# Shifted rows added in DRAM by an accumulating DMA, and the sample tile's first pages spread over four steps

## The reference

```python
proj = rms_norm(x) @ w_in            # 1024 -> 3328 columns: q, k (512 each), v (512), p (1792)
# attention group: causal differential attention, sample rows also over 512 cached rows by pages
# RWKV group:
p_prev = concat([shift0, p[:-1]])    # the row before; state_shift for the first row of a sequence
ps = p + (p_prev - p) * mu           # token shift
r, k, v, xw, xa, xg = split(ps)      # then decay, gates and the recurrence of a 64x64 state per head
h = x + concat(o_attention, o_rwkv) @ w_out
# retrieval: product keys choose 16 of 16384 experts for each of 8 heads and each row
h = h + sum_k gate_k * gelu(u[e_k] . hn) * v[e_k]
y = rms_norm(h)
```

## Time and profile before

| | |
|---|---|
| median of 3 runs | 3914.06 us (3906.76 to 3920.62) |
| the profiled execution | 3911.12 us |
| its span, first to last instruction | 3909.4 us |
| instructions | 54667 |
| busy | PE 73%, DVE 66%, POOL 35%, PEld 34%, ACT 33% |
| mean granted TensorE clock | 0.801 |
| moved by DMA | 1431.65 MB, mean 366 GB/s |

### The profile page before, as it was taken

How to read it: one execution, slowest core, us unless ns; L and a number is a source line. 1 busy time by engine, 2 the same in 40 slices (tenths; PEclk the granted TensorE clock), 3 DMA queues, 4 the chain that set the end, 5 groups by cost and what they waited for, 6 DMA issues and landing times. The chain is left out here.

```text
span 3909.4 us, 54667 instructions
## 1 busy us (share of the span) xinstructions
PE 2869.6 (73%) x20366; PEld 1341.9 (34%) x20366; DVE 2584.4 (66%) x5804; ACT 1294.6 (33%) x3597; POOL 1378.3 (35%) x1190
## 2 busy tenths in 40 slices
PE   8899999785767676767676776778676758867564
PEld 3654554342323223322332243224322315421121
DVE  2441563489578848884987598668866876446954
ACT  1321111325243424343344324432433234422222
POOL 1000000344344424443433343444333455643453
PEclk9899999787878787787878787877787767767665
DMA  7645335899999999999999999999999999999998
GB/s 253 225 149 217 138 142 196 316 420 419 423 410 420 419 422 409 411 420 420 412 414 405 419 412 392 408 418 393 394 414 390 375 361 405 408 403 422 417 400 357
DMA packets 254825, 1431.65 MB, mean 366 GB/s; under 512 B 27520, under 2 KB 45456, under 8 KB 110304
## 3 DMA queue, kind: packets, MB, share of 16 engines
q0 software_dynamic: 163232, 1162.26, 72.9%
q1 hardware_dynamic: 91328, 265.89, 18.0%
HBM read 1373.21 MB, written 54.85 MB: 365 GB/s over the span
## 5 line engine op out<-in xcount | busy, mean ns | idle before, releaser
L1039 POOL DMA_INDIRECT pe_buf<-in_experts,pe_idx x1088 | 1291.1, 1187 | 2364.9 <-PE pe_psO L1465 1637.7
L2312 DVE CUSTOM_DVE_ANT_0 pe_buf<-pe_buf,pe_hnR 128x1024 f32<-128x1024 f32 x1088 | 1316.7, 1223 | 702.2 <-DMA pe_buf<-in_experts,pe_idx 673.4
L1465 PE MATMUL pe_psO<-pe_buf,pe_Z 128*32 128x256 f32 x8704 | 847.6, 486 | 649.6 <-ACT pe_Z L1744 619.7
L1738 ACT ACTIVATE pe_gelu<-pe_dot 128x1 f32<-128x1 f32 x1088 | 219.2, 201 | 1634.4 <-DVE pe_dot L2312 1586.0
L1465 PEld LDWEIGHTS pe_psO<-pe_buf,pe_Z 128*32 128x32 f32 x8704 | 213.7, 123 | 1316.6 <-ACT pe_Z L1744 1006.0
L1447 PE MATMUL pe_psH<-pe_hn,pe_pick 128*128 128x512 f32 x544 | 409.8, 845 | 44.8 <-ACT pe_hnR L1720 39.8
L1076 PE MATMUL ip_B<-ip_w,ip_xT 128*128 128x512 f32 (+1 forms) x1008 | 426.4, 575 | 5.6 <-DMA ip_w<-in_w_in 5.6
L1744 ACT ACTIVATE pe_Z<-pe_gl,pe_gelu 128x8 f32<-128x8 f32 x1088 | 327.3, 301 | 46.4 <-issue 3.3
L1411 PE MATMUL pe_B<-op_wkr,pe_mix 128*128 128x512 f32 (+1 forms) x576 | 270.7, 615 | 7.4 <-DMA op_wkr<-scratch_wk_rows 7.0
L1076 PEld LDWEIGHTS ip_B<-ip_w,ip_xT 128*128 128x128 f32 x1008 | 190.5, 194 | 204.7 <-issue 200.3
L1447 PEld LDWEIGHTS pe_psH<-pe_hn,pe_pick 128*128 128x128 f32 x544 | 107.4, 243 | 174.9 <-issue 92.3
(11 more groups left out here) (343 smaller groups left out, 3577.6 us busy)
## 6 DMA issues: line engine op xcount, KB each, us to landing
op_wkr<-scratch_wk_rows SPq DMA_DIRECT2D x36, 2048.0 KB
ip_w<-in_w_in SPq DMA_DIRECT2D x18, 2048.0 KB, 8.3
op_w<-in_w_out SPq DMA_DIRECT2D x9, 2560.0 KB
pe_buf<-in_experts,pe_idx POOLq DMA_INDIRECT x1088
op_w<-in_w_out SPq DMA_DIRECT2D x9, 1024.0 KB
ip_w<-in_peer_wq SPq DMA_DIRECT2D x4, 2048.0 KB, 10.1
scratch_wk_rows<-wk_wkc SPq DMA_DIRECT2D x16, 512.0 KB, 3.0
tm_ps<-scratch_moved_rows SPq DMA_DIRECT2D x8, 896.0 KB
```

The source lines that it names most:

```text
L1039: pool.indirect_dma_start(buf[b][:], None, T["experts"], bass.IndirectOffsetOnAxis(ap=idx[:, t % 2, h * NJ + j:h * NJ + j + 1], axis=0)).t ...
L1465: last = nc.tensor.matmul(psO[32 * x:32 * x + 32, j // 4, :], Z[:, n % NZ, 24 - 8 * turn:56 - 8 * turn], buf[home[n]][:, D + x * QUART:D + ...
L1738: nc.scalar.activation(gelu[:, col:col + 1], dot[:, col:col + 1], ACT.Gelu_apprx_tanh).then_inc(f["gelu_done"], 1)
L2312: nc.vector.tensor_tensor_reduce(buf[b][:, 0:D], buf[b][:, 0:D], hnR[:, n // PH % 2, :], 1.0, 0.0, ALU.mult, ALU.add, dot[:, n % (NBUF + E ...
```

## The change

It has two parts.

The first adds the shifted rows in DRAM. For each projection unit with n of 3 to 6 POOL issues a DMA (`add_moved`) that reads the unit's block of `moved_rows` and adds it to the block of `kept_rows`; for the sample tile there are two, since the first row of each sequence comes from `moved_shift`. Each waits for the stores of its unit, for tile 0 also for `edge_stored`, and for the completion of all such DMAs before it (`added_of`). `load_p` is then one load of `ps` from `kept_rows`, behind the additions of its tile's last unit (`mixed_of`), all at step 25 of `op`; VectorE's addition and the semaphore value `MIXED` are gone, and three engines wait for the load itself. The sample tile's other constants are loaded at step 29, as before.

The second is about the sample tile's pages: the 16 page DMAs stand at leading steps 6, 7, 8 and 9, four in each, and the scaling of the queries at leading step 7.

```diff
+    def added_of(units):
+        return 16 * sum(1 if t < LAST else 2 for t, n in UNITS[:units] if n >= NV)
+    def mixed_of(t):
+        return added_of(last_unit(t) + 1)
...
                     if i == IP_FIRST + 2:
                         sp.wait_ge(at["lam_dots"], 1)
-                        sp.wait_ge(ip["edge_stored"], 32)
                         load_p(0)
...
             def load_p(t):
                 R = rows_of(t)
-                if t < LAST:
-                    load_moved(t)
-                    load_kept(t)
-                else:
-                    ... (p, eight blocks of ps, moved_shift, six constants)
+                sp.wait_ge(ip["mixed"], mixed_of(t))
+                sp.dma_start(ps[0:R], kept_rows[rows(t, R), :]).then_inc(s["p_in"], 16)
...
+            def add_moved(g):
+                t, n = UNITS[g]
+                cols = slice((n - NV) * IG, (n - NV) * IG + cols_of(n))
+                for i in range(2):
+                    pool.wait_ge(ip_stored[i], stored_of(g + 1, i))
+                if t == 0:
+                    pool.wait_ge(ip["edge_stored"], 32)
+                if added_of(g):
+                    pool.wait_ge(ip["mixed"], added_of(g))
+                if t < LAST:
+                    pool.dma_start(kept_rows[rows(t), cols], moved_rows[t * P:(t + 1) * P, cols], accum_op=ALU.add
+                                   ).then_inc(ip["mixed"], 16)
+                    return
+                ... (the same in two DMAs for the sample tile)
...
                 for k in range(SB_LEAD):
-                    if k == SB_LEAD - 1:
+                    if k == SB_LEAD - 4:
                         pool.wait_ge(at["pidx_ready"], 1)
                         pool.wait_ge(s["state_stored"], 32)
-                        for b in range(2):
-                            pages_of(kp, "cache_k", kp_in, b)
-                            pages_of(vp, "cache_v", vp_in, b)
+                        pages_of(kp, "cache_k", kp_in, 0)
+                    if k == SB_LEAD - 3:
+                        pages_of(vp, "cache_v", vp_in, 0)
+                    if k == SB_LEAD - 2:
+                        pages_of(kp, "cache_k", kp_in, 1)
+                    if k == SB_LEAD - 1:
+                        pages_of(vp, "cache_v", vp_in, 1)
                     yield
...
-                            dve.wait_ge(s["p_in"], 32 + 32 * t if t < LAST else 32 * PT + 160)
-                            nc.vector.tensor_tensor(ps[0:R], ps[0:R], p[0:R], ALU.add).then_inc(s["dve_part"], 1)
                         if k == 6:
-                            dve.wait_ge(s["dve_part"], ND * t + MIXED)
+                            dve.wait_ge(s["p_in"], 16 * (t + 1))
```

More of the change, by code:

```diff
@@ L313, in peer @@
     FIRST_IN, CONSTS_IN, TM_CONSTS_IN = 2, 7, 15
-    NA, ND = 9, 4
+    NA, ND = 9, 3
     LO_TANH, LO_READY, KK_SQUARED, LO_COPIED, KK_ROOT, G_COPIED, ZA_TANH, LW_READY, E_READY = range(1, 1 + NA)
-    MIXED, KK_SCALED, KK_SUM, SCALED = range(1, 1 + ND)
+    KK_SCALED, KK_SUM, SCALED = range(1, 1 + ND)
     def begin(t):
@@ L624, in peer @@
             gate_ready""")
-        ip = sems("ip", "summed squared scaled turned xT done rotated copied split mu_in shifted edge_stored")
+        ip = sems("ip", "summed squared scaled turned xT done rotated copied split mu_in shifted edge_stored mixed")
         ip_rope_in = [m.sem(f"ip_rope_in{i}") for i in range(MOST)]
@@ L753, in fold_stored, with load_sample_consts @@
                     sp.wait_ge(wk_stored[i], 16 * PH)
[L755 to L761, removed]
             def load_p(t):
                 R = rows_of(t)
-                if t < LAST:
-                    load_moved(t)
-                    load_kept(t)
-                else:
[L770 to L778, removed]
+                sp.wait_ge(ip["mixed"], mixed_of(t))
+                sp.dma_start(ps[0:R], kept_rows[rows(t, R), :]).then_inc(s["p_in"], 16)
+            def load_sample_consts():
+                for dst, n in ((sstate, "state"), (seq_of, "seq_of"), (seq_row, "seq_row"), (cum, "cum_s"), (tot, "tot_s"),
+                               (tri, "tri_s")):
+                    sp.dma_start(dst[:], T[n]).then_inc(s["sstate_in"], 16)
             def load_w_out(part):
@@ L877, in project_out @@
                         sp.wait_ge(op["hn_stored"], 16 * (t + 1))
-                        if t + 1 < LAST:
-                            load_moved(t + 1)
-                    if k == 29 and t < LAST:
+                        load_p(t + 1)
+                    if k == 29 and t + 1 == LAST:
                         sp.wait_ge(op["scores_done"], NC * t + NC - 1)
[L882 to L885, removed]
+                        load_sample_consts()
                     yield
@@ L979, in project @@
                         constants()
+                    if 2 <= i < len(IP) + 2:
+                        kind, g, q_ = IP[i - 2]
+                        if kind == "unit" and q_ == 1 and UNITS[g][1] >= NV:
+                            add_moved(g)
                     yield
+            def add_moved(g):
[11 more added lines that the diff above has]
+                    return
+                kept = kept_rows[rows(LAST, SROWS), cols].rearrange("(b s) n -> b s n", s=ST)
+                moved = moved_rows[1 + SEQ:1 + SEQ + SROWS, cols].rearrange("(b s) n -> b s n", s=ST)
+                pool.dma_start(kept[:, 1:ST, :], moved[:, 0:ST - 1, :], accum_op=ALU.add).then_inc(ip["mixed"], 16)
+                pool.dma_start(kept[:, 0, :], moved_shift[:, cols], accum_op=ALU.add).then_inc(ip["mixed"], 16)
             def mix_in_time(t):
@@ L1142, in mix_in_time @@
                             pe.wait_ge(s["act_part"], NA * t + LW_READY)
-                            pe.wait_ge(s["dve_part"], ND * t + MIXED)
+                            pe.wait_ge(s["p_in"], 16 * (t + 1))
                             nc.tensor.matmul(B[0:R, 0, :], cum[0:R, 0:R], lw[0:R, :], start=True, stop=True)
@@ L1532, in mix_in_time @@
                         if k == 6:
-                            act.wait_ge(s["dve_part"], ND * t + MIXED)
+                            act.wait_ge(s["p_in"], 16 * (t + 1))
                             nc.scalar.activation(lo[0:R, 0:64], ps[0:R, 3 * W:3 * W + 64], ACT.Tanh)
@@ L2126, in attend_sample @@
                                               ).then_inc(at["copied"], 1)
-                    yield
-                for k in range(SB_STEPS * (SB - 1) + SB_LONG):
-                    if k == 0:
+                    if k == 7:
                         dve.wait_ge(at["turned"], 2 * NT)
@@ L2137, in attend_sample @@
                         last.then_inc(at["copied"], 1)
+                    yield
+                for k in range(SB_STEPS * (SB - 1) + SB_LONG):
                     for b in range(SB):
```

## The result

The changed kernel takes 3922.50 us in the median of 20 runs (3916.96 to 3932.32), the kernel before 3907.14 in 20 runs (3897.70 to 3920.62): a ratio of 1.0039, interval 1.0032 to 1.0045, and a difference of 15.4 us. The change makes the kernel slower. The profiled execution of after took 3924.76 us with a span of 3923.0, against 3911.12 and 3909.4 before, 13.6 us more. The fill and the gather phase moved in opposite directions, each by more than I had forecast.

The account below looks back on a forecast made before the run. TensorE bounds the fill, DMA bytes the gather phase. Fold +26.0, end issues +1.1, bytes -13.2 and pages +1.5 sum to +15.4 us on 3911.1, or 3926.5, told as 3930 against the median of 3914.06; range 3906 to 3953.

Parts of the forecast that it names:

- The fold: Start of the fill: seven additions in series at 4.2 us delay tile 0's load and TensorE; +26.0 us, bounds 13.9 and 47.1.
- the end issues: End of the fill: POOL issues two additions, 0.53 us each, before its first gather; +1.1 us.
- The rival of slow additions: Fold: each addition takes 6.6 us, fold 47.1, sum +36.5 us, 3951 us; chance 0.08.
- the rival of cheap additions: Fold: an addition costs 2.6 us like POOL's small store, fold 13.9, sum +3.3 us, no change; chance 0.22.
- The Trainium skill's rule of two source reads: Additions: two source reads halve the rate, so each pays 0.6 us twice, 4 us more in the sum; not in the forecast.
- The slow stretch of TensorE: Fold: TensorE runs slow after its wait for tile 0's rows; +1.2 us, inside the fold's 26.0.
- The fill absorbs the wait: Rival: TensorE does not hang on tile 0's rows, the 26.0 us go, sum -12.6, 3901.5 us; chance 0.10.
- The bytes: Gather phase: five dropped loads of `moved_rows` save 11.0 us, the sample tile's small loads 2.2; -13.2 us in all.
- The nine small ones: Gather phase: dropping the sample tile's nine small loads, 0.46 MB, saves 2.2 us, bounds 1.1 and 6.9.
- VectorE's additions: Nine additions of 2.0 us are hidden under the DMA and give nothing; uncovered, seven in the gather phase would be 14 us.
- The pages: Sample tile's pages: POOL waits some 6 us for VectorE's indices and spreading gains nothing; +1.5 us, between 0 and +4.2.
- The rival that the dip is filled: Pages: POOL's wait costs nothing and 6.7 us of low rate come back, sum +7.2, 3921 us; chance 0.08.

Follow-up runs that it names:

- e3: Changed kernel, but the eight additions of tiles 0 and 1 don't wait for each other and tile 0's load waits for all; ratio 0.9996 to the kernel before.
- e4: Changed kernel with POOL's wait for the shifted row and its store moved out of `constants()` to fold step 2; ratio 0.9968 to the kernel before, -12.5 us.
- e8: Changed kernel with `accum_op` left out of the three DMAs, so plain copies instead of additions; 3920.05 us in one profiled run.
- e2: Changed kernel with the pages and query scaling as before, so the additions in DRAM alone; ratio 1.0047 to the kernel before, +18.4 us.
- e10: Changed kernel with the shifted row's store moved to fold step 2 and the pages back at their place of before; ratio 0.9957 to the kernel before, -16.8 us.
- e7: Kernel before without the loads of `moved_rows` for the eight prompt tiles, VectorE adding the kept part to itself; ratio 0.9960, -15.6 us.
- e6: Kernel before with one load of 64 rows in place of the sample tile's nine small loads, same bytes; ratio 0.9993, -2.7 us.
- e11: Kernel before with three more DRAM to DRAM transfers of 0.92 MB beside each load of tiles 3 to 7; ratio 1.0103, +40.2 us.
- e1: Kernel before with only the change's second part, pages at leading steps 6 to 9 and query scaling at step 7; ratio 1.0012, +4.7 us.
- e9: Changed kernel with the shifted row's store moved to fold step 2 and the pages at steps 9 to 12; 3887.94 us, ratio 0.9937 to the kernel before.
- e12: Kernel before with only the pages moved to steps 9 to 12 and query scaling at step 7; ratio 0.9998, -0.8 us.

## Why the prediction was right

Slower by 15.4 us was forecast and measured, but the match of the sums is luck: the fill came out 7.3 us dearer than forecast, and the bytes gave back as much more, which is beyond the bounds that I had set for them.

- **The fold** (forecast 26.0, with the end issues 27.1; measured 34.4). The mechanism held at each link, and e3 and e4 show it by taking one link each. The sizes were low. At ScalarE's first use the delay is 173.62 - 142.63 = 31.0 for my 24.8: 1.1 because everything from POOL's last constant on ran that much later, 0.6 of waiting in front of the first addition, 3.4 in seven steps (32.5 against 29.1) and 1.2 in the load (173.62 - 168.05 = 5.6 against 4.4). The step that was off is the price of an addition: I built 4.2 from a small load of 3.4 and the bytes. e8 gives a copy of 3.5 us a step, so the adding makes it 4.65. The rival of slow additions, 6.6 us each, fell with that as well. Against the mean of the five untouched fills (727.2) the first gather of after is 33.7 us late, so 34.4 is good to about 1.
- **The Trainium skill's formula** for one DMA of GpSimd (DMA: Bandwidth & Descriptors, section Anatomy of one DMA — SWDGE (gpsimd) path) gave an estimate of 2.6 us for 256 KB and gives 2.3 for 128 KB. The copies of e8, 2.9 and 2.3, are near it. The additions, 4.3 and 3.3, are not, and so the rival of cheap additions fell. The Trainium skill's rule of two source reads (Collectives: The Full Stack, section The bandwidth ceiling: the fold count and why AG ≠ RS ≠ AR) has the sign right: by my estimate it asks for 0.6 us more at 256 KB and half that at 128 KB, the runs show 1.4 and 1.0. From 128 to 256 KB the difference grows by 0.4, about what the second read would add; a line through these two sizes leaves some 0.6 that does not grow. POOL's longer issue could be 0.3 of that; neither is tested.
- **The slow stretch of TensorE** (forecast +1.2). It is there, and larger: TensorE did nothing in the wait, the granted clock fell from 1.00 at its start to 0.50 (1.2 GHz) in its second half, stayed there from 174.6 to 179.8 with TensorE busy, and was 1.00 (2.4 GHz) again from 181. Eight products of L1118 take 2.08 us in it, where 8 took 1.16 just ahead of the wait. From the first product on tile 0's rows to that of L1152 it is 5.2 us in after and 2.6 before (L1138), so 2.6 on the spot for my 1.2. But it can't be found in the sum. From TensorE's first product on tile 0's rows to the first gather it is 582.2 us before, 586.3 in after, 584.4 in e3, which has the same 2.08 and loses 2.1 on the spot, and 583.6 in e4, which has no wait. Two end issues (2.1 us: 758.73 to 760.86, not 1.1) and a scatter of about 2 are all that this shows.
- **The fill absorbs the wait** (chance 0.10): refuted. From SP's load to the first gather after, e3 and e4 take 592.8, 590.9 and 590.9 us, for loads that lie up to 29 us apart. The shift goes through whole.
- **The bytes** (forecast -13.2, bounds -12.1 and -17.9). The profiled gather phases differ by 20.8; by the medians it is 34.4 - 15.4 = 19.0, and without the 1.5 of the pages the bytes gave 20.5. The other kernels with the additions give, as the shift of their first gather less that of their median, 14 (e2), 17 (e3, e4) and 21 (e10), with the 1.5 of the pages added in e3 and e4, so 18 in the mean of the five. What e7 and e6 give together is near that: 15.6 + 2.7, and 1.1 for the 0.46 MB that e6 keeps, an estimate at 418 GB/s, makes 19.4. The loads were mis-sized: five of them are worth 15.6 by e7 and 13.5 by the 2.7 of e11, for my 11.0. The nine small ones are worth 3.8 with that 1.1 (0.3 to 7.7) for my 2.2, and VectorE's additions nothing, as said. Why a load costs 2.7 and not the 2.2 of its bytes is open.
- **The pages** (forecast +1.5): measured +1.5 in after and in e1, +1.4 in e4 (-22.4 to -21.0), with the wait of 6.26 us for my "some 6"; against the mean of the kernels with the pages as before it is 2.4. What the whole part costs by medians (+4.7 in e1, 4.3 between e10 and e4, less than nothing between e2 and after) is as uncertain as it is large. The rival that the dip is filled fell in this form. That the place was the fault and not the spreading is what the shifts over the pages in e9 and e12 say (-3.5 and -2.7); the totals don't settle it.

My list of what would make me wrong named a gather phase shorter by over 20 us. The profiles show 20.8, the medians 19.0: it is the bytes term which stood at that edge, by its size and not by its mechanism.

## What to carry to other kernels

Where a change adds DMAs to a queue, look at which wait the queue stands in when they become ready: here one store at the end of `constants()` at 132 us, first read at 669, held back eight additions, the first of which could go at 80, and a chain in series at 4.65 us a link then stood in front of the engine that bounds the fill. Moved behind the work that doesn't need it, the same wait turned +15 us into -12.5, and into -25 with the pages behind their indices, though how much of that last step is theirs isn't settled. The page DMAs that were put ahead of their input held up POOL's gathers for 6.26 us and brought nothing.

## What the hardware did that I had not expected

- A DRAM to DRAM addition of 256 KB lands in 4.3 us and its copy in 2.9; 128 KB in 3.3 and 2.3. POOL issues an addition in 0.81 us and a copy in 0.53.
- Additions overlap well: eight were issued in 6.78 us and done 13.9 us after the first began, 1.7 us each against 4.65 in series.
- A transfer of 0.92 MB in the saturated phase costs 2.7 us (2.3 to 3.1), not the 2.2 of its bytes at the 418 GB/s of an undisturbed stretch.
